# Low weight parts of the search stage made by GpSimd alone, and four re-orderings around it

## The chip, the cores and the metric

The kernel is one program on one core of a Trainium2 chip. The time is the device time of an execution in microseconds (us). TensorE (PE, with its weight loads PEld), VectorE (DVE), ScalarE (ACT), GpSimd (POOL) and SyncE (SP, which only issues DMAs here) each run their own instructions in order and wait for each other through semaphores.

## The reference

Two layers of a token model, 256 tokens by 1024 features, all in float32. Layer 0 has a gated MLP (w_in, w_out), layer 1 a pooling mixer (p_in, p_out); each is followed by an expert block. Cut to what matters:

```
mod = silu(c) @ ada_w[i] + ada_b[i]              # 6 chunks: shift, scale, gate, twice
h   = rmsnorm(x) * gain * (1 + scale) + shift
q   = h @ w_q                                    # 1024 -> 8 heads x 2 x 128
s1, s2 = q_half1 @ k1.T, q_half2 @ k2.T          # 128 scores each
v1, i1 = top_k(s1, 16);  v2, i2 = top_k(s2, 16)
best, pos = top_k(v1[:, None] + v2[None, :], 16) # experts i1 * 128 + i2
out = sum_k gelu(h . u[e_k]) * softmax(best)_k * v[e_k]
```

The kernel computes gelu(h . u[e]) for all 16384 experts, masks the result with the gates of the chosen ones, and multiplies with all of v.

## The kernel before

All weights stream through TensorE as tiles of 128 x 1024 float32 (512 KB), in the order w_v, w_u, w_out, w_q, u, v for layer 0 and p_in, p_out, w_q, u, v for layer 1. A product runs in a reduced float32 form, so each tile is split: `wH` is ScalarE's copy of `raw` (line 403), `wL = raw - wH` is the low part. In most stages VectorE makes the first half of `wL` (`low_first`, line 627) and GpSimd the second (`low_second`, line 382); in the second band of u and in v VectorE makes it whole (`low_tile`, line 633). `raw`, `wH` and `wL` have four buffers each: SyncE loads tile n when TensorE has finished tile n - 4. ScalarE copies three tiles ahead, VectorE two (`ahead`, `ahead_whole`). TensorE's `tile_product` (lines 1185 to 1187) takes 24 matmuls for a tile: wH by hH, wH by hL, wL by hH for each of 8 k; `first_two` (lines 1200 to 1202) is the same for the first two tiles of a stage, right behind a norm.

**The front.** 16 tiles of ada_w are scaled by silu(c) and added on VectorE (`ada_front`, lines 646 and 649), eight for the scale chunk and eight for the shift chunk. TensorE sums the partitions (`modulations`, line 1228) and takes the mean square of x (`mean`, line 1218). `inverse_root` is line 686, `scaled` line 689, `low_h` line 694. The other chunks' 80 tiles of ada_w are loaded and added among later stages; `ADA_W_V` and `ADA_W_OUT` say behind which tiles.

**The search.** u has 128 tiles in two bands of 64. During the first band VectorE searches the best keys and experts: 66 steps (`topk_step`), of which 0 to 22 search single scores, 23 to 38 the sums C (line 934 makes C), 39 and 40 convert, 41 to 64 are eight groups of two products and a sum (lines 960, 968, 970) and 65 normalises the gates. `share` gives each step a price and spreads the steps between the `low_first` of the 64 tiles. ScalarE takes the exponential behind tile 52, TensorE transposes the result ahead of tile 60 (`stage(..., 60, BAND)`).

**The bands.** In the second band of u, and in the first half of v, VectorE, ScalarE and TensorE also mask the first and second band of results R (`gate_step`, `multiply`, line 1013). A masked tile of R is split in its turn: `gateH` on ScalarE (line 555, `split_gated`) and `gateL` on VectorE (line 1110, `low_gated`), both of which `values` needs for a v tile.

Of the kernel before, what the change touches and what calls it, by code (L numbers as in the profile page):

```python
# [27 lines left out]
KT = D // P  # L28
# [14 lines left out]
EXP_TILES = KEYS  # L43
RAW = 4
# [19 lines left out]
def build(nc, xt_d, c_d, ada_d, adab_d, n1_d, n2_d, fg_d, w_in_d, vg_d, ws_d, bs_d, w_out_d, p_in_d, p_grp_d,  # L64
# [13 lines left out]
    with ctx:  # L78
# [127 lines left out]
        s_low = sem("s_low")  # L206
        s_pe = sem("s_pe")
# [65 lines left out]
        ADA_W_OUT = tuple(t for t in range(4, 16) if t % 3 != 0)  # L273
# [6 lines left out]
        HALVES = (0, BASE["p_in", 1] - BASE["u", 0] - BAND)  # L280
        WHOLE = (BASE["u", 0] + BAND, BASE["u", 1] + BAND - (BASE["p_in", 1] - BASE["u", 0] - BAND))
# [3 lines left out]
        def _(sp):  # L285
# [34 lines left out]
            for t in range(16):  # L320
                load(stream_dram["w_u", 0], W_U, t // 4, t % 4)
                if t < 4:
                    load_ada(ada_s, m)
                    m += 1
# [43 lines left out]
        def _(pool):  # L368
# [15 lines left out]

            for layer in range(LAYERS):
                base, end = (0, BASE["p_in", 1])[layer], BASE["u", layer] + BAND
                with pool.Fori(0, (end - base) // 4) as i:
                    for s in range(4):
                        low_second(layer, base, i, s)
                if layer == 0:  # L390
# [8 lines left out]
        def _(act):  # L399
# [40 lines left out]
            nc.scalar.activation(csT[:, :], csT[:, :], ACT.Silu).then_inc(s_silu, 1)  # L440
            act.wait_ge(s_x, 16)
# [4 lines left out]
            for layer in range(LAYERS):  # L446
# [74 lines left out]
                experts(0, 52)  # L521
# [3 lines left out]
                experts(52, BAND)  # L525
# [85 lines left out]
        def _(dve):  # L611
# [148 lines left out]
            for layer in range(LAYERS):  # L760
                if layer == 0:
# [27 lines left out]
                    for t in range(16):  # L789
                        ahead(W_U, t // 4, t % 4)  # L790
                        if t < 4:
# [124 lines left out]
                for t in range(16):  # L916
                    ahead(BASE["w_q", layer], t // 4, t % 4)
# [124 lines left out]
                def share(n):  # L1042

                    if n < 39:
                        return (17, 24)[n > 22] + (14 if n == 0 else 28 if n in (23, 31) else 0)
                    return 12 if n < 41 or n == 65 else (7, 7, 12)[(n - 41) % 3]

                base = BASE["u", layer]
                made = 0
# [20 lines left out]
                dve.wait_ge(s_bank_a, 4 + ACT_EVACS + ACT_PER_LAYER * layer + 16 + BAND)  # L1070
                def whole_sum(i, s):
# [34 lines left out]
                def low_gated(i, s):  # L1106

                    dve.wait_ge(s_gH2, 4 * i + (layer * EXP_TILES + s + 1))
                    gated = ds(4 * i + s, 1)
                    nc.vector.tensor_tensor(gateL[s % 4][:, :],  # L1110
# [58 lines left out]
        def _(pe):  # L1169
# [100 lines left out]
            for j in range(KT):  # L1270
                mean(0, j)
# [240 lines left out]
```

## Time and profile before

| | us |
|---|---|
| median of 3 runs | 1999.16 (1992.68 to 2001.68) |
| profiled execution | 2005.55 |
| its span, first to last instruction | 2003.8 |
| TensorE busy in the span | 1920.3 |
| mean granted TensorE clock | 0.979 of full speed |

The profiled execution is 6.4 us over the median of the runs, and 1.75 us of it lie outside the span. All times below count from the start of the span. A matmul's time in the trace overlaps with the next one's, so a group's mean is longer than its pace.

### The profile page before, as it was taken

What the parts mean: (1) busy time and instruction counts of PE and PEld (TensorE: products, weight loads), DVE (VectorE), ACT (ScalarE), POOL (GpSimd) and SP (SyncE); (2) the same over time, 40 slices, a digit from 0 to 9 for tenths busy, and PEclk for the clock granted to TensorE, in tenths of its full rate; (3) what the DMA queues carried; (4) which work ended last, traced back from release to release, by engine and by line L of the source; (5) the groups of instructions that cost most, each with busy time, mean ns of one, the idle gap of its engine ahead of it and who ended that gap; (6) DMA issues with size and microseconds to landing.
All of it is one profiled execution on the core that took longest, in us unless ns stands there. A gap on an engine that the chain in (4) does not pass through costs nothing.

```text
span 2003.8 us, 40366 instructions
## 1 busy us (share of the span) xinstructions
PE 1920.3 (96%) x14140; PEld 1717.9 (86%) x14140; DVE 1597.5 (80%) x2713; ACT 921.1 (46%) x1470; POOL 346.6 (17%) x237
## 2 busy tenths in 40 slices
PE   3999899999999999999999899999999999999998
PEld 3999899999888888878888899999888878887886
DVE  7757588997998888888996558897898888886555
ACT  3464344454454444444543344444555544444454
POOL 1544344441000000000002344444000000000000
PEclk8999899999999999999997999999999999999999
DMA  7846345556554455568883335555664445545553
GB/s 285 314 158 232 125 150 185 170 168 203 197 184 160 151 167 167 167 229 318 323 302 116 127 137 168 178 177 169 210 201 157 166 156 167 167 166 177 194 189 136
DMA packets 104179, 376.38 MB, mean 188 GB/s; under 512 B 12464, under 2 KB 12464, under 8 KB 103856
## 3 DMA queue, kind: packets, MB, share of 16 engines
q1 hardware_dynamic: 103680, 373.43, 54.8%
q0 software_dynamic: 432, 2.10, 0.3%
q8 instruction: 38, 0.62, 0.1%
q14 instruction: 29, 0.24, 0.0%
HBM read 374.43 MB, written 1.05 MB: 187 GB/s over the span
## 4 chain that ended last, share of the span: by engine, by line
PE 84%; DVE 8%; DMA 4%; ACT 1%; issue 1%; SPq 0%; DVEq 0%; ACTq 0%
PE ring L1381 12%; PE O L1415 12%; PE O L1417 11%; PE O L1416 11%; PE ring L1185 8%; PE ring L1187 7%; PE ring L1186 7%; PE ring L1383 6%; PE ring L1357 2%; PE O L1357 2%; DVE wL L627 2%; DMA raw<-in_u 1%; PE O L1228 1%; PE O L1218 1%; DMA raw<-in_v 1%
## 5 line engine op out<-in xcount | busy, mean ns | idle before, releaser
L403 ACT ACTIVATE wH<-raw 128x1024 fp32r<-128x1024 f32 x608 | 644.8, 1061 | 982.2 <-DMA raw<-in_v 397.2
L633 DVE TENSOR_TENSOR wL<-raw,wH 128x1024 fp32r<-128x1024 f32 x384 | 469.8, 1223 | 195.4 <-ACT wH L403 193.3
L1185 PE MATMUL ring<-hX,wH 128*128 128x256 f32 x1536 | 444.6, 289 | 11.0 <-DVE wL L627 11.0
L1186 PE MATMUL ring<-hX,wH 128*128 128x256 f32 x1536 | 437.6, 285 | 0.0
L1187 PE MATMUL ring<-hX,wL 128*128 128x256 f32 x1536 | 437.5, 285 | 0.0
L382 POOL TENSOR_TENSOR wL<-raw,wH 128x512 fp32r<-128x512 f32 x224 | 343.7, 1536 | 466.7 <-ACT wH L403 466.5
L1415 PE MATMUL O<-wH,gateH 128*128 128x512 f32 x1024 | 408.4, 399 | 7.0 <-DVE gateL L1110 6.8
L1417 PE MATMUL O<-wH,gateL 128*128 128x512 f32 x1024 | 401.7, 392 | 0.0
L1416 PE MATMUL O<-wL,gateH 128*128 128x512 f32 x1024 | 400.7, 391 | 0.0
L1381 PE MATMUL ring<-hX,wH 128*128 128x512 f32 x1024 | 367.9, 402 | 0.0
L1185 PEld LDWEIGHTS ring<-hX,wH 128*128 128x128 f32 x1536 | 296.8, 193 | 14.7 <-DVE wL L627 10.9
L1186 PEld LDWEIGHTS ring<-hX,wH 128*128 128x128 f32 x1536 | 296.7, 193 | 0.1
L1187 PEld LDWEIGHTS ring<-hX,wL 128*128 128x128 f32 x1536 | 296.4, 193 | 0.0
L627 DVE TENSOR_TENSOR wL<-raw,wH 128x512 fp32r<-128x512 f32 x224 | 204.5, 917 | 108.2 <-ACT wH L403 107.1
L1383 PE MATMUL ring<-hX,wL 128*128 128x256 f32 x1024 | 287.2, 280 | 0.0
L1415 PEld LDWEIGHTS O<-wH,gateH 128*128 128x128 f32 x1024 | 193.6, 189 | 47.4 <-DVE gateL L1110 5.2
L1381 PEld LDWEIGHTS ring<-hX,wH 128*128 128x128 f32 x1024 | 192.7, 188 | 42.7
L1417 PEld LDWEIGHTS O<-wH,gateL 128*128 128x128 f32 x1024 | 193.4, 189 | 41.4
L1416 PEld LDWEIGHTS O<-wL,gateH 128*128 128x128 f32 x1024 | 194.0, 189 | 38.6
L1383 PEld LDWEIGHTS ring<-hX,wL 128*128 128x128 f32 x1024 | 194.0, 189 | 0.0
L1004 DVE TENSOR_TENSOR oneA<-oneE,selG 128x1536 bf16<-128x1536 bf16 x128 | 121.7, 951 | 0.3
L1110 DVE TENSOR_TENSOR gateL<-R,gateH 128x256 fp32r<-128x256 f32 x256 | 106.4, 417 | 7.2 <-ACT gateH L555 7.2
(168 smaller groups left out, 1952.9 us busy)
## 6 DMA issues: line engine op xcount, KB each, us to landing
raw<-in_u SPq DMA_DIRECT2D x256, 512.0 KB, 3.3
raw<-in_v SPq DMA_DIRECT2D x256, 512.0 KB, 3.3
ada_v<-in_ada SPq DMA_DIRECT2D x40, 512.0 KB, 4.7
raw<-in_w_in SPq DMA_DIRECT2D x32, 512.0 KB, 4.1
raw<-in_w_q SPq DMA_DIRECT2D x32, 512.0 KB, 3.3
ada_f<-in_ada SPq DMA_DIRECT2D x16, 512.0 KB, 10.5
ada_s<-in_ada SPq DMA_DIRECT2D x16, 512.0 KB, 4.8
raw<-in_w_out SPq DMA_DIRECT2D x16, 512.0 KB, 3.5
```

The lines of the kernel that those rows point to most:

```text
L382: nc.gpsimd.tensor_tensor(wL[s % RAW][:, HALF:], raw[s % RAW][:, HALF:], wH[s % RAW][:, HALF:].bitcast(fp32), ALU.subtract).then_inc(s_l1, 1)
L403: nc.scalar.activation(wH[s % RAW][:, :], raw[s % RAW][:, :], ACT.Copy).then_inc(s_h, 1)
L627: nc.vector.tensor_tensor(wL[s % RAW][:, 0:HALF], raw[s % RAW][:, 0:HALF], wH[s % RAW][:, 0:HALF].bitcast(fp32), ALU.subtract).then_inc(s_ ...
L633: nc.vector.tensor_tensor(wL[s % RAW][:, :], raw[s % RAW][:, :], wH[s % RAW][:, :].bitcast(fp32), ALU.subtract).then_inc(s_low, 1)
L1185: mm(bank[:, 0:T], a, xH[:, k0 + k, :], start=(first and k == 0), stop=False)
L1186: mm(bank[:, 0:T], a, xL[:, k0 + k, :], start=False, stop=False)
L1187: ins = mm(bank[:, 0:T], b, xH[:, k0 + k, :], start=False, stop=(last and k == KT - 1))
L1381: mm(bank[:, :], wH[s][:, k * P:k * P + P], hX[:, k, :, :].rearrange("p two t -> p (two t)"), start=(k == 0), stop=False)
L1383: ins = mm(bank[:, 0:T], wL[s][:, k * P:k * P + P], hH[:, k, :], start=False, stop=(k == KT - 1))
L1415: mm(o[:, :], a, high, start=first, stop=False)
L1416: mm(o[:, :], a, low, start=False, stop=False)
L1417: ins = mm(o[:, :], b, high, start=False, stop=last)
```

## The change

The diff, cut to its core:

```diff
-        ADA_W_OUT = tuple(t for t in range(4, 16) if t % 3 != 0)
+        ADA_W_OUT = (4, 5, 7, 8)
+        SEARCH = 48
@@ sync and vector, in the w_u stage: four more ada tiles @@
-                if t < 4:
+                if t < 8:
@@ gpsimd @@
+            pool.wait_ge(s_acc, ADA_FRONT)
+            def low_whole(base, i, s):
+                pool.wait_ge(s_h, 4 * i + (base + s + 1))
+                nc.gpsimd.tensor_tensor(wL[s % RAW][:, :], raw[s % RAW][:, :], wH[s % RAW][:, :].bitcast(fp32),
+                                        ALU.subtract).then_inc(s_low_p, 1)
             for layer in range(LAYERS):
-                base, end = (0, BASE["p_in", 1])[layer], BASE["u", layer] + BAND
+                base, end = (0, BASE["p_in", 1])[layer], BASE["u", layer]
                 (low_second for tiles base to end, as before)
+                with pool.Fori(0, SEARCH // 4) as i:
+                    for s in range(4):
+                        low_whole(end, i, s)
@@ scalar: front, exponential, end of the second band @@
             nc.scalar.activation(csT[:, :], csT[:, :], ACT.Silu).then_inc(s_silu, 1)
+            act.wait_ge(s_const, 6)
+            warm_root()
...
-                experts(0, 52)
+                experts(0, 40)
                 act.wait_ge(s_diff, layer + 1)
                 nc.scalar.activation(best[:, :, :, :], ex[:, :, :, :], ACT.Exp).then_inc(s_exp, 1)
                 warm()
-                experts(52, BAND)
+                experts(40, BAND)
...
                 for s in range(4):
-                    act.wait_ge(s_sum, BAND * layer + 4 * last + s)
-                    ahead(BASE["u", layer] + BAND, last, s)
-                    gelu(last, s - 1)
                     if s == 3:
                         act.wait_ge(s_gated, NGRP * (2 * layer + 1))
                         split_gated(0, 0, first=True)
                         split_gated(0, 1, first=True)
+                    act.wait_ge(s_sum, BAND * layer + 4 * last + s)
+                    gelu(last, s - 1)
+                    ahead(BASE["u", layer] + BAND, last, s)
@@ vector: front @@
             modulations(1, (1,), O[3], (0,))
+            for m in range(KT + 3, ADA_FRONT):
+                ada_front(m)
             dve.wait_ge(s_x, 16)
             inverse_root(0)
-            for m in range(KT + 3, ADA_FRONT):
-                ada_front(m)
@@ vector: w_q and search @@
-                    ahead(BASE["w_q", layer], t // 4, t % 4)
+                    if t < 14:
+                        ahead(BASE["w_q", layer], t // 4, t % 4)
...
-                for n in range(BAND):
-                    if n < BAND - 2:
-                        ahead(base, n // 4, n % 4)
-                    else:
-                        ahead_whole(base, n // 4, n % 4)
-                    while made < 66 and sum(share(x) for x in range(made + 1)) <= 19 * (n + 2):
-                        topk_step(made)
-                        made += 1
+                for n in range(66):
+                    topk_step(n)
+                for n in range(SEARCH - 2, BAND):
+                    ahead_whole(base, n // 4, n % 4)
@@ vector: end of the second band, then of v's first half @@
                 for s in range(4):
+                    if s == 3:
+                        whole_sum(PAIRS - 1, s - 1)
+                        low_gated(0, 0)
+                        low_gated(0, 1)
                     ahead_whole(base + BAND, PAIRS - 1, s)
-                    whole_sum(PAIRS - 1, s - 1)
-                    gate_step(PAIRS - 1, s, 0, last=True)
+                    if s < 3:
+                        whole_sum(PAIRS - 1, s - 1)
+                        gate_step(PAIRS - 1, s, 0, last=True)
-                low_gated(0, 0)
-                low_gated(0, 1)
...
                     else:
+                        if s == 3:
+                            low_gated(PAIRS, 0)
                         ahead_whole(base, PAIRS - 1, s)
                     gate_step(PAIRS - 1, s, 1, last=True)
-                low_gated(PAIRS, 0)
                 low_gated(PAIRS, 1)
@@ tensor: front, search stage @@
+            modulations(acc_f, 0, 1, KT, O[3])
             for j in range(KT):
                 mean(0, j)
-            modulations(acc_f, 0, 1, KT, O[3])
             modulations(acc_f, 1, 2, ADA_FRONT, O[3][:, KT:])
...
-                stage("u", layer, s_bank_a, before, 0, 60)
+                stage("u", layer, s_bank_a, before, 0, SEARCH, by_pool=layer)
+                stage("u", layer, s_bank_a, before, SEARCH, 60, whole=layer)
...
-                stage("u", layer, s_bank_a, before, 60, BAND)
+                stage("u", layer, s_bank_a, before, 60, BAND, whole=layer)
```

With `by_pool` and `whole`, `tile_product` waits once for the whole low part, where it waited for each half. The constants that count the semaphores follow.

First place, VectorE in the front, before. `acc_f` are the sums of ada_w, `rstd` the inverse root, `sq` the scaled x:

```order
L649 SCALAR_TENSOR_TENSOR acc_f<-ada_f,csT,acc_f 128x1024 x2
L675 TENSOR_TENSOR mod<-O,adab 128x8
L679 SCALAR_TENSOR_TENSOR gs<-mod,n 128x8
L682 MEMSET tick 128x1
L686 RECIPROCAL rstd<-std 128x256
L649 SCALAR_TENSOR_TENSOR acc_f<-ada_f,csT,acc_f 128x1024 x5
L689 SCALAR_TENSOR_TENSOR sq<-XT,gs,rstd 128x256 x4
```

The same place of the changed kernel:

```order
L664 SCALAR_TENSOR_TENSOR acc_f<-ada_f,csT,acc_f 128x1024 x2
L690 TENSOR_TENSOR mod<-O,adab 128x8
L694 SCALAR_TENSOR_TENSOR gs<-mod,n 128x8
L697 MEMSET tick 128x1
L664 SCALAR_TENSOR_TENSOR acc_f<-ada_f,csT,acc_f 128x1024 x5
L701 RECIPROCAL rstd<-std 128x256
L704 SCALAR_TENSOR_TENSOR sq<-XT,gs,rstd 128x256 x4
```

The reciprocal stands behind the last five sums, where it stood ahead of them.

Second place, VectorE in the search, layer 0, before; `M` is the comparison matrix of steps 41 to 64:

```order
L627 TENSOR_TENSOR wL<-raw,wH 128x512
L960 TENSOR_TENSOR M<-ab,iota_b 128x1024
L968 TENSOR_TENSOR M<-M,top_f 128x1024
L627 TENSOR_TENSOR wL<-raw,wH 128x512
L970 TENSOR_REDUCE sel<-M 128x64
L960 TENSOR_TENSOR M<-ab,iota_b 128x1024
```

The last such group of the changed kernel and what follows it:

```order
L984 TENSOR_TENSOR M<-M,top_f 128x1024
L986 TENSOR_REDUCE sel<-M 128x64
L991 TENSOR_REDUCE zsum<-best 128x16
L992 RECIPROCAL zsum<-zsum 128x16
L993 TENSOR_TENSOR sel<-best,zsum 128x256
L648 TENSOR_TENSOR wL<-raw,wH 128x1024 x17
L1069 CAST selK<-O 128x512 x2
```

The low parts are gone from between the steps, and whole ones come in a row behind the last step.

Third place, VectorE at the end of the second band, before. Line 1075 is `whole_sum`:

```order
L1013 TENSOR_TENSOR R<-O,R 128x64x8 x2
L633 TENSOR_TENSOR wL<-raw,wH 128x1024
L1075 TENSOR_TENSOR R<-ring,R 128x256
L1110 TENSOR_TENSOR gateL<-R,gateH 128x256 x2
L1075 TENSOR_TENSOR R<-ring,R 128x256
```

And changed:

```order
L1029 TENSOR_TENSOR R<-O,R 128x64x8 x2
L1088 TENSOR_TENSOR R<-ring,R 128x256
L1080 TENSOR_TENSOR gateL<-R,gateH 128x256 x2
L648 TENSOR_TENSOR wL<-raw,wH 128x1024
L1088 TENSOR_TENSOR R<-ring,R 128x256
```

The two `gateL` stand ahead of the last low part of the band, where they stood behind it.

## Rows read from the trace of the kernel before

**Rows 1.** The page's first part: busy time, share of the span and instructions of each engine.
```profile
PE 1920.3 (96%) x14140; PEld 1717.9 (86%) x14140; DVE 1597.5 (80%) x2713; ACT 921.1 (46%) x1470; POOL 346.6 (17%) x237
```

**Rows 2.** TensorE's waits over the span: us in total, times, longest us.
```profile
PE ring L1185 <- DVE wL L627: 13.2, 16, 2.2
PE O L1228 <- DVE acc_f L649: 11.7, 1, 11.7
PE O L1415 <- DVE gateL L1110: 6.8, 4, 2.4
```

**Rows 3.** TensorE's waits in 300:480, then in 1210:1400.
```profile
PE ring L1185 <- DVE wL L627: 4.5, 6, 1.2
...
PE ring L1185 <- DVE wL L627: 4.2, 5, 1.2
```

**Rows 4.** Timeline of 205:214, TensorE at the end of w_out.
```profile
210.17 1.92 PE L1228 MATMUL O<-ones,acc_s 128*128 128x1 f32 x16 [1.67 <-DVE acc_s L649]
```

**Rows 5.** Timeline of 18:43: start us, us, engine, line, work, [idle before].
```profile
19.94 2.67 DVE L649 SCALAR_TENSOR_TENSOR acc_f<-ada_f,csT,acc_f 128x1024 f32<-128x1024 f32 x2 [0.52 <-DMA ada_f<-in_ada]
...
25.63 1.75 DVE L686 RECIPROCAL rstd<-std 128x256 f32<-128x256 f32 x1
27.41 9.38 DVE L649 SCALAR_TENSOR_TENSOR acc_f<-ada_f,csT,acc_f 128x1024 f32<-128x1024 f32 x5
...
30.04 5.68 POOL L382 TENSOR_TENSOR wL<-raw,wH 128x512 fp32r<-128x512 f32 x3 [28.16 <-ACT wH L403]
...
36.72 1.66 DVE L689 SCALAR_TENSOR_TENSOR sq<-XT,gs,rstd 128x256 f32<-128x256 f32 x4
...
36.85 3.57 PE L1228 MATMUL O<-ones,acc_f 128*128 128x1 f32 x16 [11.75 <-DVE acc_f L649]
38.31 1.28 DVE L627 TENSOR_TENSOR wL<-raw,wH 128x512 fp32r<-128x512 f32 x2
...
42.03 0.55 PE L1200 MATMUL ring<-hX,wH 128*128 128x256 f32 x1 [1.60 <-DVE hX L694]
```

**Rows 6.** Busy time in windows: 286:343; 277:445; 277:445, VectorE's L627 alone; 107:121.
```profile
286.00:343.00 57.00, 57.00 (x477) 57.00 (x476) 52.53 (x188) 26.61 (x41) 26.47 (x20) 1.00 0.55 184
...
277.00:445.00 168.00, 163.54 (x1335) 162.01 (x1335) 149.85 (x396) 77.47 (x116) 78.75 (x56) 0.99 0.51 169
...
277.00:445.00 168.00, 51.07 (x55) 0.99 0.51 169
...
107.00:121.00 14.00, 14.00 (x121) 14.00 (x120) 4.40 (x5) 10.58 (x23) 7.25 (x5) 1.00 0.50 161
```

**Rows 7.** Timeline of 674:680, where the second band ends in layer 0.
```profile
674.05 1.28 DVE L1013 TENSOR_TENSOR R<-O,R 128x512 f32<-128x512 f32 x2
...
678.67 0.71 ACT L555 ACTIVATE gateH<-R 128x256 fp32r<-128x256 f32 x2
```

**Rows 8.** Timeline: GpSimd alone, then beside VectorE, from 355 on.
```profile
358.45 1.30 POOL L382 TENSOR_TENSOR wL<-raw,wH 128x512 fp32r<-128x512 f32 x1 [1.43 <-ACT wH L403]
...
438.33 1.84 POOL L382 TENSOR_TENSOR wL<-raw,wH 128x512 fp32r<-128x512 f32 x1 [3.17 <-ACT wH L403]
...
438.32 0.69 DVE L960 TENSOR_TENSOR M<-ab,iota_b 128x1024 bf16<-128x1024 bf16 x1
439.05 1.67 DVE L627 TENSOR_TENSOR wL<-raw,wH 128x512 fp32r<-128x512 f32 x1
```

**Rows 9.** The page: ScalarE's weight copies (part 5) and the loads (part 6).
```profile
L403 ACT ACTIVATE wH<-raw 128x1024 fp32r<-128x1024 f32 x608 | 644.8, 1061 | 982.2 <-DMA raw<-in_v 397.2
...
raw<-in_u SPq DMA_DIRECT2D x256, 512.0 KB, 3.3
```

**Rows 10.** VectorE's groups by shape in 268:455: busy us, mean ns | idle before.
```profile
L970 DVE TENSOR_REDUCE sel<-M 128x64 f32<-128x1024 bf16 x8 | 9.7, 1214 | 0.1
...
L934 DVE TENSOR_TENSOR C<-top_v 128x2048 f32<-128x2048 f32 x2 | 6.8, 3384 | 0.0
```

**Rows 11.** Timeline of ScalarE in 279:295: the result of the search's first tile leaves.
```profile
282.01 0.38 ACT L516 ACTIVATE R<-ring 128x256 f32 x1 [2.81 <-PE ring L1187]
```

More of the change, by code:

```diff
@@ L206, in build @@
         s_low = sem("s_low")
+        s_low_p = sem("s_low_p")
         s_pe = sem("s_pe")
@@ L277, in build @@
         ACT_PER_LAYER = 16 + EXP_TILES
-        HALVES = (0, BASE["p_in", 1] - BASE["u", 0] - BAND)
-        WHOLE = (BASE["u", 0] + BAND, BASE["u", 1] + BAND - (BASE["p_in", 1] - BASE["u", 0] - BAND))
+        SEARCH = 48
+        HALVES = (0, BASE["p_in", 1] - BASE["u", 0])
+        BY_POOL = (BASE["u", 0], BASE["u", 1] - SEARCH)
+        WHOLE = (BASE["u", 0] + SEARCH, BASE["u", 1] + SEARCH - (BASE["p_in", 1] - BASE["u", 0] - SEARCH))
         @block.sync
@@ L790, in _ @@
                         ahead(W_U, t // 4, t % 4)
-                        if t < 4:
+                        if t < 8:
                             ada_tile(ada_s, acc_s, m // KT - 2, m)
@@ L1040, in gate_step @@
                         multiply(i, 0, band)
[L1042 to L1046, printed above, removed]
                 base = BASE["u", layer]
-                made = 0
-                for n in range(BAND):
-                    if n < BAND - 2:
-                        ahead(base, n // 4, n % 4)
-                    else:
-                        ahead_whole(base, n // 4, n % 4)
-                    while made < 66 and sum(share(x) for x in range(made + 1)) <= 19 * (n + 2):
-                        topk_step(made)
-                        made += 1
+                for n in range(66):
+                    topk_step(n)
+                for n in range(SEARCH - 2, BAND):
+                    ahead_whole(base, n // 4, n % 4)
                     if n == 62:
@@ L1070, in _, with low_gated @@
                 dve.wait_ge(s_bank_a, 4 + ACT_EVACS + ACT_PER_LAYER * layer + 16 + BAND)
+                def low_gated(i, s):
+                    dve.wait_ge(s_gH2, 4 * i + (layer * EXP_TILES + s + 1))
+                    gated = ds(4 * i + s, 1)
+                    nc.vector.tensor_tensor(gateL[s % 4][:, :],
+                                            R[:, gated, :].rearrange("p a t -> p (a t)"),
+                                            gateH[s % 4][:, :].bitcast(fp32), ALU.subtract).then_inc(s_gL2, 1)
                 def whole_sum(i, s):
@@ L1099, in _ @@
                 for s in range(4):
+                    if s == 3:
+                        whole_sum(PAIRS - 1, s - 1)
+                        low_gated(0, 0)
+                        low_gated(0, 1)
                     ahead_whole(base + BAND, PAIRS - 1, s)
-                    whole_sum(PAIRS - 1, s - 1)
-                    gate_step(PAIRS - 1, s, 0, last=True)
+                    if s < 3:
+                        whole_sum(PAIRS - 1, s - 1)
+                        gate_step(PAIRS - 1, s, 0, last=True)
                 base = BASE["v", layer]
[L1106 to L1110, printed above, removed]
-                                            R[:, gated, :].rearrange("p a t -> p (a t)"),
-                                            gateH[s % 4][:, :].bitcast(fp32), ALU.subtract).then_inc(s_gL2, 1)
                 def ahead_gated(i, s):
@@ L1170, in _, with tile_product @@
             mm = nc.tensor.matmul
-            def tile_product(base, i, s, bank, xH, xL, k0=0, first=True, last=True, pairs=None, whole=None):
+            def tile_product(base, i, s, bank, xH, xL, k0=0, first=True, last=True, pairs=None, whole=None, by_pool=None):
                 if whole is not None:
                     pe.wait_ge(s_low, 4 * i + (base - WHOLE[whole] + s + 1))
+                if by_pool is not None:
+                    pe.wait_ge(s_low_p, 4 * i + (base - BY_POOL[by_pool] + s + 1))
                 for k in range(KT):
-                    if whole is None and k % 4 == 0:
+                    if whole is None and by_pool is None and k % 4 == 0:
                         pe.wait_ge((s_l0, s_l1)[k // 4], 4 * i + (base - HALVES[base >= BASE["p_in", 1]] + s + 1))
@@ L1204, in first_two, with stage @@
                             ins.then_inc(s_pe, 1)
-            def stage(name, layer, emptied, before, lo=0, hi=None):
+            def stage(name, layer, emptied, before, lo=0, hi=None, **made):
                 base = BASE[name, layer]
@@ L1212, in stage @@
                         pe.wait_ge(emptied, 4 * i + (before + s + 1))
-                        tile_product(base, i, s, ring[s], hH, hL)
+                        tile_product(base, i, s, ring[s], hH, hL, **made)
             def mean(n, j):
```

## The prediction

> **What bounds the kernel now.** I read the page first: TensorE is busy 1920.3 us of the span [rows 1], so the most that any re-ordering can give is the 83 us in which it stands. Then TensorE's waits, to see whom it waits for: VectorE's half low parts 13.2 us in 16 waits, the front's sums of ada_w 11.7 us in one, `gateL` 6.8 us in four [rows 2]. The same view by stretch puts 4.5 us of the low-part waits into the search of layer 0 and 4.2 us into that of layer 1 [rows 3]; the rest is in w_v, w_u and w_out, where the low parts stay as they are. Last the timelines around those waits. The change touches 11.7 + 6.8 + 8.7 us of waiting, and a 1.67 us wait at the end of w_out [rows 4].
>
> **The front.** Before, VectorE takes the reciprocal at 25.63, five sums from 27.41 (9.38 us), four scaled tiles (1.66), two low halves (1.28); TensorE's second sums over partitions run from 36.85 for 3.57 and end at 40.42, and the first product starts 1.61 later, at 42.03 [rows 5]. The five sums took 1.88 each, where the two before them took 1.33: GpSimd's three halves of 30.04 to 35.72 lay beside them [rows 5]. After: TensorE sums the scale chunk while it would wait for x, so VectorE goes on at 22.6 (19.94 + 2.67) with 0.5 of small operations, ends five undisturbed sums at 23.1 + 5 x 1.39 = 30.05 (1.33 and a gap), then reciprocal 1.75, scaled 1.66, low halves 1.28: 34.7. GpSimd now starts at 30.05, by its new wait, so its three halves (3.9 alone) lie beside the scaled tiles and the low halves. What VectorE loses to it is bounded by nothing and by all 3.9; I take 1.9, since the reciprocal has one input and ran undisturbed, and half of GpSimd's work falls there. That is 36.6. TensorE's second sums end at 30.05 + 3.57 = 33.6, ahead of it. The first product starts at 36.6 + 1.6 = 38.2 and the front gains 3.8, between 1.8 and 5.7. The mean squares start some 2.5 us later than before, but the root is not asked for until 30.05: no cost. The square-root table is loaded early, off the path too.
>
> **The sums spread.** Four additions move from w_out to w_u. In 107:121 VectorE is busy 4.40 of 14 us [rows 6]; four sums at 1.3 to 2.3 us add 5 to 9 us there and fit. Their four loads move with them on SyncE's queue, each behind a weight load and each waiting for an earlier sum; the next weight load stands behind that wait, and it is short as long as VectorE has this room. At the end of w_out TensorE stops at 208.5 and starts its sums at 210.17, 1.67 later [rows 4]; with the additions done long before, it goes straight on: 1.7 gained. If the cover in w_u fails, each sum holds up a low half by up to 1 us: 0 to 2 us lost; I take 0.
>
> **The gate tiles.** At the end of the second band both masks are done at 674.05 + 1.28 = 675.3, but ScalarE makes `gateH` only at 678.67, behind a weight copy that waits for its load [rows 7]. After, ScalarE waits for the masks first, with the last weight copy of the stage behind that wait, and they are done before it gets there: `gateH` follows at about 675.9 and `gateL` at 676.7; TensorE ends its tile at 677.4, so the whole wait goes. The low part behind it is done at 678.3, and TensorE wants it one v tile later, at 680. In the middle of v `gateL` is made ahead of a low part that waits for ScalarE. All four waits go: 6.8 gained.
>
> **The search.** Removed: 48 of VectorE's halves per layer, and with them the waits of [rows 3], 8.7 us. Added: GpSimd makes 48 whole parts. Is it fast enough? TensorE does 477 matmuls in 57 us, so a tile of 24 takes 2.87 [rows 6]. GpSimd's half takes 1.30 alone [rows 8]; a whole one lies between 1.30 (nothing for more columns) and 2.60 (twice), and near the latter: I take 2.45, since some of 1.30 is start-up. The Trainium skill, page "GPSIMD Engine Reference", section 3.1, gives about 2.6 cycles at 1.2 GHz per element for a two-input operation, 2.2 us here as an estimate and some start-up, which would leave the sum as it is, and it says to leave elementwise work to VectorE; no run here yet shows a whole tile. So GpSimd keeps up by 0.4 us a tile. The latency: a tile's load starts when TensorE is four tiles ahead, and three tiles (8.6 us) later it is wanted. Load 3.3, copy 1.06 [rows 9], GpSimd 2.45 and some 0.5 of hand-over make 7.3: a slack of 1.3.
>
> What eats it is the port that GpSimd and VectorE share in operations with two inputs. At 438.3 VectorE's M product and GpSimd's half start together: GpSimd takes 1.84 in place of 1.30; then VectorE's next, of 0.69 alone, takes 1.67 and ends 0.55 after GpSimd's end [rows 8]. One waits for the other, and about 0.13 us of each overlap. In steps 41 to 64 there are 16 M products. A GpSimd tile and one of them take 2.45 - 0.13 + 0.55 = 2.87 per tile: GpSimd just holds TensorE's pace, and VectorE gets one product in per tile. Price: 0.2 to 0.5 us for each of the two C products (3.4 us [rows 10], against a slack of 1.3), about 0.3 for ScalarE's exponential behind tile 40, 0 to 1.5 for the M products. By the Trainium skill, "SBUF — State Buffer", section "SBUF: two separate sides", the pair is an exclusive lock for the whole instruction; without the overlap a pair would take 3.14, GpSimd would fall back 16 x 0.27 = 4.3 us, and 3 us a layer would come back as waits. The trace agrees that one blocks the other, with the 0.13 less at each end.
>
> Is VectorE in time for tile 48, which it makes itself? Its work in 277:445 is 149.85, less 51.07 for low halves 98.8 [rows 6], and about 5 more to the last step: 104 us from 277 on. The M products wait for GpSimd's tiles: 16 x 2.87 = 46 us, where eight groups of 0.69 + 0.69 + 1.21 [rows 8, 10] take 21; that adds 25, the conversions ahead of them about 5. The last step ends at about 411, between 406 and 417. Tile 0 ends at about 282.0 [rows 11], so tile 48 is wanted at 282.0 + 47 x 2.87 = 416.9, and its part must start by 415.7. It holds, by little; a miss costs 0 to 2 us. In all I give back 1.3 us a layer: the search gains 8.7 - 2.6 = 6.1, between 0 and 8.7.
>
> **The sum.** 3.8 + 1.7 + 6.8 + 6.1 = 18.4 us. The profiled execution of 2005.55 would be 1987.2; the median of the runs, 6.4 lower, goes from 1999.16 to 1980.8.
>
> **The rivals.**
> Port: the lock costs GpSimd and VectorE more than I took: a pair of whole tile and M product takes 3.1 us or more, and the search ends behind tile 48. Then waits of 4 to 5 us a layer come back, in the last third of the first band, the search gains nothing, and 12.3 us remain: 1986.9. For it: the two estimates above are both within 1 to 5 us of tipping. Against: the pair in the rows, and GpSimd's 0.4 us of room wherever no such product comes.
> Front: all of GpSimd's 3.9 us stand in VectorE's way, and the front gives 1.8 only: 16.4 in all, 1982.8. This lies within the likeliest case's range.
> GpSimd too slow, the one on the other side: a whole low part takes more than a tile of TensorE, and 96 tiles pay the difference. The rest gains 12.3 and the removed waits 8.7, so it breaks even at 2.87 + 21/96 = 3.09 and at 3.3 the kernel is 20 us slower: 2019. For it: the 56 halves of 277:445 took 1.41 each [rows 6], and twice that is 2.81, 0.06 short of a tile. Against: those include halves that stood beside VectorE's own half, which is no longer there; alone it is 1.30 [rows 8].
> Nothing: the waits only move to the next semaphore. Every engine behind them (loads 3.3 us, copies 1.06) has more slack than the waits are long, so I give it little: within 5 us of before, 1996.
>
> **Chances.** Likeliest 0.66 (1974 to 1988), port 0.20, GpSimd too slow 0.07, nothing 0.07. 0.5% is 10 us, about what a measurement of this kernel can tell from no change (its three runs spread over 9 us). Faster by more: the first two cases, less the part of them above 1989: 0.80. Slower: the part of the third beyond 3.2 us a tile: 0.05. The rest, 0.15, is no change. The range takes in the first two cases and the width of the runs: 1971 to 1991.
>
> **What would show it.** GpSimd's whole parts at 2.4 to 2.6 us alone and 2.9 to 3.1 beside M products; the M products at up to 3 us each; waits of TensorE in the search under 3 us a layer; no wait for `gateL`; the first product at about 38 us; no wait for `acc_s` at the end of w_out. Wrong would be: GpSimd busy without a gap through tiles 0 to 47 and TensorE waiting for it tile by tile; or a wait of more than 3 us at tile 48.

## The result and the profile after

The changed kernel takes 1971.35 us (median of four runs, 1968.64 to 1976.10) against 1999.41 of the kernel before: a ratio of 0.9871, interval 0.9847 to 0.9896. A repetition in another call gave 1970.78 and 0.9864 (0.9844 to 0.9884). The profiled execution went from 2005.55 to 1976.1, its span from 2003.8 to 1973.9. The forecast was 1980.8, 9.4 us above the median: the medians gained 28.1 us where 18.4 were forecast. All four terms have the right sign.

TensorE's waits over the span, in the columns of [rows 2]:

```profile
PE O L1239 <- DVE acc_f L664: 20.3, 2, 17.2
PE ring L1211 <- DVE hX L709: 16.8, 4, 4.4
PE O L1275 <- ACT UV L522: 5.9, 6, 2.0
PE ring L1196 <- DVE wL L642: 2.6, 2, 2.1
...
PE O L1229 <- ACT sq L423: 1.6, 1, 1.6
PE ring L1196 <- POOL wL L392: 0.8, 2, 0.5
```

The 13.2 us for VectorE's low halves have become 2.6, 2.1 of it at the start of w_out, GpSimd's whole parts (`low_whole`, L392) cost 0.8, and `gateL` and `acc_s` are gone. The 20.3 for `acc_f` isn't new time: its 17.2 lies at the start, where TensorE waited for x before. The page has TensorE busy for 1914.6 us, 5.7 less than in [rows 1], with as many matmuls; a re-ordering alone does not explain that, and it is followed up below.

The front (timeline of 19:43), beside [rows 5]:

```profile
23.23 6.84 DVE L664 SCALAR_TENSOR_TENSOR acc_f<-ada_f,csT,acc_f 128x1024 f32<-128x1024 f32 x5
...
29.99 1.75 DVE L701 RECIPROCAL rstd<-std 128x256 f32<-128x256 f32 x1
30.13 3.58 PE L1239 MATMUL O<-ones,acc_f 128*128 128x1 f32 x16 [3.15 <-DVE acc_f L664]
30.32 3.92 POOL L385 TENSOR_TENSOR wL<-raw,wH 128x512 fp32r<-128x512 f32 x3 [28.43 <-ACT wH L416]
...
31.77 3.54 DVE L704 SCALAR_TENSOR_TENSOR sq<-XT,gs,rstd 128x256 f32<-128x256 f32 x4
35.24 1.28 DVE L642 TENSOR_TENSOR wL<-raw,wH 128x512 fp32r<-128x512 f32 x2
...
38.00 0.55 PE L1211 MATMUL ring<-hX,wH 128*128 128x256 f32 x1 [4.29 <-DVE hX L709]
```

The five sums take 6.84 in place of 9.38 and end at 30.07 (forecast 30.05). The scaled tiles take 3.54, 1.88 more than the 1.66 of [rows 5], because GpSimd's 3.92 lie beside them (forecast 1.9), and the first product starts at 38.00 (forecast 38.2).

The search in layer 0: GpSimd's parts (min/median/max ns, first and last start), then VectorE's groups in 362:406 (busy us, mean ns), then the timeline, GpSimd beside the last M products and VectorE where the search ends:

```profile
L392 POOL TENSOR_TENSOR wL<-raw,wH x47: 2363/2411/4445, 263.6 to 404.0; 128x1024 fp32r<-128x1024 f32 x47
```
```profile
L984 DVE TENSOR_TENSOR M<-M,top_f 128x1024 bf16<-128x1024 bf16 x8 | 20.2, 2519 | 0.3
L976 DVE TENSOR_TENSOR M<-ab,iota_b 128x1024 bf16<-128x1024 bf16 x8 | 12.6, 1570 | 0.3
L986 DVE TENSOR_REDUCE sel<-M 128x64 f32<-128x1024 bf16 x8 | 9.8, 1220 | 0.3
```
```profile
393.14 13.67 POOL L392 TENSOR_TENSOR wL<-raw,wH 128x1024 fp32r<-128x1024 f32 x5 [2.04 <-ACT wH L416]
...
406.57 0.52 DVE L993 TENSOR_TENSOR sel<-best,zsum 128x256 f32<-128x256 f32 x1
407.01 1.22 DVE L648 TENSOR_TENSOR wL<-raw,wH 128x1024 fp32r<-128x1024 f32 x1
```

GpSimd's whole part takes 2.41 us where nothing hinders it (taken: 2.45). The Trainium skill's 2.2 us and some start-up (page "GPSIMD Engine Reference", section 3.1, an estimate from its cycles per element) agrees. Of two M products, 0.69 each when alone [rows 8], one takes 1.57 and the other 2.52 on average: VectorE pays more for the port than GpSimd. The last step ends at 407.09 (forecast 411, bounds 406 to 417).

**Where the time came from.** I cut every execution at the same events: the starts of ScalarE's table loads, and the start of norm 1's root. "experts0" and "experts1" are the stretches with u and v, search included, of layer 0 and layer 1. The rows of the repetition of the changed kernel (timeline of ScalarE):

```profile
40.59 1.28 ACT L447 ACT_TABLE_LOAD   x1
...
155.17 1.28 ACT L450 ACT_TABLE_LOAD   x1
...
266.85 1.28 ACT L447 ACT_TABLE_LOAD   x1
...
1040.45 1.28 ACT L450 ACT_TABLE_LOAD   x1
...
1187.68 1.28 ACT L447 ACT_TABLE_LOAD   x1
...
1950.09 1.28 ACT L450 ACT_TABLE_LOAD   x1
```

The lengths between them, in us. "Low clock" is what TensorE lost below its full clock after 40 us, summed from windows of 4 us as busy time x (1 - granted clock), windows at 0.985 or more left out. A time "cleared of the clock" is a length less this sum over its windows:

```
                   front w_v,w_u  w_out  to u  experts0 between experts1   span  low clock
before, recorded    44.4  118.1   50.7   63.5   784.8    149.1   773.1   2003.8   28.7
before, repeated    45.5  116.1   51.7   62.2   782.3    146.4   772.0   1996.1   18.0
after, recorded     40.4  116.2   48.6   62.9   773.7    150.0   762.0   1973.9   23.8
after, repeated     40.6  114.6   48.8   62.9   773.6    147.2   762.4   1969.9   16.5
e1 gate tiles old   40.6  113.6   48.9   63.0   776.6    146.8   766.5   1975.9   18.0
e2 search old       40.6  113.6   48.7   63.3   779.0    145.0   766.7   1976.8   15.2
e3 front old        44.7  114.1   48.8   63.2   773.0    146.8   762.6   1972.9   18.2
e4 sums old         40.6  113.4   51.6   62.4   773.2    145.6   762.3   1969.0   15.0
e10 front+sums old  43.6  114.8   51.6   63.8   774.0    145.9   763.5   1977.1   19.0
```

Two executions of one kernel differ by 10.7 and 7.3 us in the last column alone, and the 5.7 us of TensorE's busy time above are mostly its 4.9. Without it the recorded pair gains 2003.8 - 28.7 - (1973.9 - 23.8) = 25.0 and the repeated one 1996.1 - 18.0 - (1969.9 - 16.5) = 24.7. That they agree so well is chance: with the low clock off, the two executions of before still differ by 3.0 us and those of the changed kernel by 3.3, and the pairs taken crosswise give 21.7 and 28.0. So the gain is 25 us, give or take 3, against a sum of 18.4.

### The profile page after: what moved, and what is told of

Same layout as the page of the kernel before. It is cut to its first block, busy times and chain, and to the rows that moved or that the text cites. A ratio compares the mean times of both kernels' runs of the same rounds, so it can differ in the third digit from the quotient of the medians.

```text
span 1973.9 us, 40165 instructions
## 1 busy us (share of the span) xinstructions
PE 1914.6 (97%) x14140; PEld 1716.5 (87%) x14140; DVE 1572.1 (80%) x2617; ACT 921.8 (47%) x1471; POOL 404.5 (20%) x205
## 4 chain that ended last, share of the span: by engine, by line
PE 60%; issue 19%; POOL 14%; DVE 3%; DMA 2%; ACT 1%; SPq 0%; POOLq 0%; DVEq 0%; ACTq 0%
PE O L1427 12%; PE O L1429 11%; PE O L1428 11%; PE ring L1393 10%; POOL wL L392 9%; POOL wL L385 6%; PE ring L1395 5%; PE ring L1368 2%; PE ring L1196 2%; PE ring L1197 2%; PE ring L1198 2%; PE O L1368 2%; DMA raw<-in_u 1%; ACT wH L416 1%; DVE wL L648 1%
## 5 line engine op out<-in xcount | busy, mean ns | idle before, releaser
L648 DVE TENSOR_TENSOR wL<-raw,wH 128x1024 fp32r<-128x1024 f32 x416 | 508.7, 1223 | 232.0 <-ACT wH L416 230.8
L392 POOL TENSOR_TENSOR wL<-raw,wH 128x1024 fp32r<-128x1024 f32 x96 | 246.3, 2576 | 47.1 <-ACT wH L416 46.7
L1428 PEld LDWEIGHTS O<-wL,gateH 128*128 128x128 f32 x1024 | 193.0, 188 | 38.2
L385 POOL TENSOR_TENSOR wL<-raw,wH 128x512 fp32r<-128x512 f32 x96 | 155.3, 1621 | 254.6 <-ACT wH L416 254.6
L642 DVE TENSOR_TENSOR wL<-raw,wH 128x512 fp32r<-128x512 f32 x96 | 88.0, 920 | 67.1 <-ACT wH L416 66.9
```

The costliest lines, as they stand in the source:

```text
L385: nc.gpsimd.tensor_tensor(wL[s % RAW][:, HALF:], raw[s % RAW][:, HALF:], wH[s % RAW][:, HALF:].bitcast(fp32), ALU.subtract).then_inc(s_l1, 1)
L392: nc.gpsimd.tensor_tensor(wL[s % RAW][:, :], raw[s % RAW][:, :], wH[s % RAW][:, :].bitcast(fp32), ALU.subtract).then_inc(s_low_p, 1)
L648: nc.vector.tensor_tensor(wL[s % RAW][:, :], raw[s % RAW][:, :], wH[s % RAW][:, :].bitcast(fp32), ALU.subtract).then_inc(s_low, 1)
L1428: mm(o[:, :], a, low, start=False, stop=False)
```

## The experiments

Each is the changed kernel but for the edit shown. In the first group e1, e2, e3 and e4 put one part back and e10 two; e9 adds work to e1; r_before and r_after are the two kernels unchanged. The expected totals of e1, e2, e3 and e9 were counted from the recorded 1976.1, and the repetition's median is 1970.78, so they are some 5 us high by that alone. Above that median stand e1 by 7.6 us, e2 by 9.2, e3 by 5.2, e4 by 3.7 and e10 by 6.1. The ratios of e3, e4 and e10 overlap the repetition's, so what these cost is read from their rows and stretches.

**The parts, one by one.**

```diff
# e1 (VectorE; ScalarE's split_gated likewise behind its gelu)
-                    if s == 3:
-                        whole_sum(PAIRS - 1, s - 1)
-                        low_gated(0, 0)
-                        low_gated(0, 1)
...
+                low_gated(0, 0)
+                low_gated(0, 1)
```

> The changed kernel with the gate tiles back behind the weight copies (ScalarE and VectorE). Theory 'wait and clock': TensorE's four waits for gateL come back (2.2 to 2.4 us at the start of v, 1.0 to 1.2 in its middle, both layers, 6.8 in sum) and behind each of the two longer ones the granted clock falls to about 0.57 for 4 us, as in the trace of before, with some 12 matmuls in those 4 us where the changed kernel has 19 to 21: 1.7 us more a layer. Together 10 us: the profiled execution goes from 1976.1 to 1986 and the gain from the first v product to 8 tiles later is 1.7 smaller in each layer. Rival 'wait alone': the same waits, 6.8 us, 1983, and the clock at 1.00 in the first 4 us of v.

Measured: 1978.42 us, ratio 0.9913 (0.9895 to 0.9931). The waits, and the start of v in layer 0 (windows: busy times and matmul counts, granted clock after POOL):

```profile
PE O L1423 <- DVE gateL L1080: 6.7, 4, 2.4
```
```profile
659.00:663.00 4.00, 2.03 (x12) 1.53 (x10) 1.49 (x3) 2.18 (x6) 0.00 (x0) 1.00 0.53 161
663.00:667.00 4.00, 3.58 (x16) 2.97 (x17) 3.14 (x7) 2.88 (x7) 0.00 (x0) 1.00 0.21 85
```

The four waits are back with 6.7 us and the expert stages are 3.0 and 4.1 longer than the repetition's, 7.1 in all. Of the 3.0, 2.3 is low clock elsewhere in the stretch, where the repetition has none and the recorded execution 1.8; cleared of it, e1 costs 4.8 us against the repetition and 6.9 against the recorded execution. The clock behind the wait of 2.4 is 1.00, and so it is in layer 1. The rival holds: the wait alone.

```diff
# e9 = e1 and, ahead of the first v product
+                pe.wait_ge(s_h, base + 1)
+                for _ in range(9):
+                    mm(O[2][:, :], wH[0][:, 0:P], wH[0][:, 0:HALF], start=True, stop=True)
```

> The kernel of e1 with nine matmuls of 128x128x512 on the first v tile's own high part ahead of the first v product, so that TensorE is at work through the wait for gateL; they are started and stopped for themselves, and the product overwrites their bank. (Work is added, the result is the same.) Theory 'wait and clock': v still starts as late as in e1, but the clock stays at 1.00 in its first 4 us, so it is about 3.4 us faster than e1 (1982 to 1983 against 1986). Rival 'wait alone', the low rate of matmuls in those 4 us has another cause (low parts or banks): e9 is as long as e1, or 1 to 3 us longer.

Measured: 1985.81 us, ratio 0.9945 (0.9927 to 0.9963), 7.4 more than e1; the spans differ by 2.4 (1978.3 and 1975.9), and in them the expert stages (777.1 and 768.0) by 0.5 and 1.5, with waits for low parts of 1.5 us (VectorE's) and 1.3 (GpSimd's) that e1 has not. Two of the executions without a profile, 1986.0 and 1989.5 us, were granted 0.984 of the clock, where the profiled one of 1980.5 had 0.987. Keeping TensorE at work through the gap bought nothing, as there was no fall of the clock to avoid.

> The kernel before once more, unchanged, for its granted clock. In the recorded execution the clock stood at 0.57 in the 4 us behind both waits for gateL at the start of v (2.2 and 2.4 us long); in e1, with waits of 2.4 and 2.3 us at the same place, it stood at 1.00. Theory 'it follows from the kernel': 0.5 to 0.7 again in both layers here. Rival 'it varies from execution to execution, as the stretches behind the norms do (0.5 to 0.95 in the same places)': 1.00 in at least one of the two layers, and the time at low clock, 28.7 us of loss in the recorded execution, is 15 to 25 here.

The same windows, first of the recorded execution of before, then of this one:

```profile
676.00:680.00 4.00, 1.83 (x11) 1.35 (x10) 1.72 (x5) 2.24 (x5) 0.00 (x0) 1.00 0.52 187
680.00:684.00 4.00, 4.00 (x12) 3.13 (x11) 3.14 (x7) 1.98 (x4) 0.00 (x0) 0.57 0.04 17
684.00:688.00 4.00, 4.00 (x19) 3.31 (x18) 2.23 (x3) 0.71 (x2) 0.00 (x0) 1.00 0.37 131
```
```profile
673.00:677.00 4.00, 1.61 (x11) 1.17 (x9) 2.08 (x4) 2.95 (x8) 0.00 (x0) 1.00 0.53 179
677.00:681.00 4.00, 4.00 (x18) 3.33 (x19) 3.14 (x7) 2.43 (x6) 0.00 (x0) 1.00 0.09 38
```

The kernel and the gap (2.2 and 2.4 us) are the same; one execution falls to 0.57 and does 12 matmuls in 4 us, the other stays at 1.00 and does 18. The rival holds: it varies from execution to execution. That is 7/19 of 4 us or 1.5 in each layer of the recorded pair, which the change can save but doesn't always.

> The changed kernel once more, unchanged, on the chip of this call, to set the experiments against. Theory: the stretches between the landmarks (266 to 1042 and 1190 to 1956) repeat within 1 us (773.7 and 762.0 us), the ratio is 0.985 to 0.990, and the clock loss of 23.8 us in the recorded execution is smaller here by some us, since the four kernels of the first call showed 15 to 18. Rival: the clock loss is the same 24 and belongs to the kernel.

Measured: 773.6 and 762.4, within 0.4 us of the recorded ones; ratio 0.9864; loss at low clock 16.5. The theory holds.

```diff
# e2 (the pieces of it)
-        SEARCH = 48
-                with pool.Fori(0, SEARCH // 4) as i:
-                    for s in range(4):
-                        low_whole(end, i, s)
-                for n in range(66):
-                    topk_step(n)
+                    while made < 66 and sum(share(x) for x in range(made + 1)) <= 19 * (n + 2):
+                        topk_step(made)
+                        made += 1
```

> The changed kernel with the search as before: VectorE and GpSimd make a half of each low part each, and the search's steps lie between them by the table of shares. The prediction gave this part 6.1 us (8.7 of waits less 2.6 given back). The two traces give 4.8 in layer 0 and 5.5 in layer 1. Theory 'nothing is given back, and the removed waits cost more than their length': 9 to 11 us slower than the changed kernel, 1985 to 1987, with 4 to 5 us of waits for wL in each search. Rival 'the 6.1 of the prediction was right and the rest of the gain came from elsewhere in the stretch': 6 us slower, 1982.

Measured: 1979.97 us, ratio 0.9912 (0.9885 to 0.9938); expert stages 5.4 and 4.3 longer than in the repetition, 9.7 in all (cleared of the clock 8.4, and 10.5 against the recorded execution). TensorE's waits in 262:430, 1185:1350 and 1350:1410:

```profile
PE ring L1199 <- DVE wL L637: 4.7, 6, 0.9
...
PE ring L1199 <- DVE wL L637: 2.4, 3, 0.9
...
PE ring L1199 <- DVE wL L637: 1.2, 2, 0.7
```

These are 8.3 us, near the 8.7 of [rows 3]. The changed kernel pays 0.8 of it at most. So the part is worth 8 to 10 us and not 6.1: the theory holds, the forecast's give-back of 2.6 didn't come.

```diff
# e3 (VectorE; no wait of GpSimd for the sums; ScalarE and TensorE in the old order likewise)
-            for m in range(KT + 3, ADA_FRONT):
-                ada_front(m)
             dve.wait_ge(s_x, 16)
             inverse_root(0)
+            for m in range(KT + 3, ADA_FRONT):
+                ada_front(m)
# e4
-        ADA_W_OUT = (4, 5, 7, 8)
+        ADA_W_OUT = tuple(t for t in range(4, 16) if t % 3 != 0)
-                        if t < 8:
+                        if t < 4:
```

> The changed kernel with the front in its old order, on all four engines: GpSimd's halves beside the five sums, the reciprocal ahead of them, TensorE's scale chunk after the mean squares. Prediction: the first product 3.8 us later than in the changed kernel (41.8 against 38.0). The traces give 4.0. Rival, since layer 1 gave back 0.9 in its front: the front is worth only 3 by the end of the program. Total 1979 to 1980.

> The changed kernel with the eight modulation sums of w_out back in w_out (none of the four in w_u). Prediction: 1.7 us slower by the end of w_out, one wait for acc_s of about 1.7 us. The traces of before and after show 1.8 more in w_v and w_u, where low-part waits fell from 2.4 to 0.6. Theory A (these waits come from the sums too): 3 to 4 us slower by norm 1's root (landmark 205). Rival B (they come from something else, such as GpSimd's later start in the front): 1.7 slower, w_v and w_u unchanged.

> The changed kernel with front and modulation sums both as before, because 1.5 us of the gain in w_v and w_u (cleared of the granted clock) came back in no single experiment. Theory 'each alone hides it, both bring it': 40 to 157 (from the front's table load to that of w_out) takes 113.2 to 114.1 us cleared of the clock, as before, and not 111.3 to 112.0. Rival 'it belongs to neither': 111.3 to 112.0 again, and the whole kernel is the sum of e3 and e4, 4.1 + 2.8 = 6.9 us slower than the changed one.

Measured: e3 1976.0 us, ratio 0.9899 (0.9882 to 0.9917), front 4.1 longer, nothing else moved. e4 1974.44 us, 0.9889 (0.9866 to 0.9913), w_out 2.8 longer, and its wait is

```profile
PE O L1239 <- DVE acc_s L664: 1.9, 1, 1.9
```

with w_v and w_u as they are in the changed kernel: rival B. Its whole span is 0.9 shorter than the repetition's, within what two executions differ by, so the 2.8 rests on the stage alone. e10 1976.84 us, 0.9895 (0.9879 to 0.9912), front 3.0 and w_out 2.8 longer, the span 7.2. Its w_v and w_u take 114.8 less 2.5 at low clock, 112.3, between the 111.3 to 112.0 of the others and the 113.2 to 114.1 of before, so neither theory is met. No part that I put back brings this last 1 to 2 us whole.

**GpSimd's speed.**

```diff
# e7 (8 parts of 128 columns; the other run: 4 of 256)
-                nc.gpsimd.tensor_tensor(wL[s % RAW][:, :], raw[s % RAW][:, :], wH[s % RAW][:, :].bitcast(fp32),
-                                        ALU.subtract).then_inc(s_low_p, 1)
+                for q in range(0, KT * P, 128):
+                    ins = nc.gpsimd.tensor_tensor(wL[s % RAW][:, q:q + 128], raw[s % RAW][:, q:q + 128],
+                                                  wH[s % RAW][:, q:q + 128].bitcast(fp32), ALU.subtract)
+                ins.then_inc(s_low_p, 1)
```

> The changed kernel with each whole low part of GpSimd cut into four instructions of 256 columns (same result). From the rows, 512 columns take 1.30 and 1024 take 2.41, so 0.19 of it is start-up: four take about 2.95 us a tile, against 2.87 of TensorE. Theory 'GpSimd must stay below TensorE's tile, and every tile above it pays the difference' (the prediction's rival 'GpSimd too slow'): 96 x 0.08 = 8 us slower than the changed kernel less the lead it starts with (about 1 us a layer), so 5 to 8 us slower, with waits of TensorE for GpSimd's low parts in both searches. Rival 'the port's lock gives way between instructions, so shorter ones let VectorE in and the search keeps its time': within 2 us of the changed kernel.

> The same with eight instructions of 128 columns: by the rows 8 x 0.47 = 3.7 us a tile. Theory as above: 96 x 0.83 = 80 us slower less some us of lead, so about 2045, slower than the kernel before (the price per tile of the rival 'GpSimd too slow'); TensorE waits 0.8 us for GpSimd at each of 48 tiles a layer. If the start-up overlaps between instructions on one queue, the four and the eight parts both stay near 2.4 us a tile and both runs stay within 2 us of the changed kernel.

Measured: 1987.61 us, ratio 0.9952 (0.9936 to 0.9969), and 2038.11 us, ratio 1.0205 (1.0186 to 1.0225). GpSimd's group by shape, and TensorE's wait for it, of the four parts and then of the eight:

```profile
L393 POOL TENSOR_TENSOR wL<-raw,wH 128x256 fp32r<-128x256 f32 x384 | 292.7, 806 | 14.1 <-ACT wH L418 14.0
...
PE ring L1198 <- POOL wL L393: 13.6, 21, 1.1
```
```profile
L393 POOL TENSOR_TENSOR wL<-raw,wH 128x128 fp32r<-128x128 f32 x768 | 348.4, 500 | 8.1 <-ACT wH L418 8.0
...
PE ring L1198 <- POOL wL L393: 43.4, 78, 2.3
```

A tile takes GpSimd 292.7/96 = 3.05 us and 348.4/96 = 3.63. Against the 1970.78 of the repetition the kernel loses 16.8 and 67.3 us, so 50.5 us for 96 x 0.58 more: 0.91 for each us. The waits as listed come to only 13.6 and 43.4; why they cost more is worked out below. The line through the two points, an estimate, meets zero at 3.05 - 16.8/(96 x 0.91) = 2.86 us a tile, which is TensorE's 2.87 [rows 6], and meets the kernel before (1996.35 beside these runs, 25.6 above the repetition) at 3.15, where the forecast had 3.09. The theory holds; the expected 5 to 8 us for four parts was too low, since a tile took 0.10 more than it was sized at.

**GpSimd's start in the front.**

```diff
# e5
-            pool.wait_ge(s_acc, ADA_FRONT)
+            pool.wait_ge(s_xn, 4)
```

> The changed kernel with GpSimd's start behind the four scaled tiles instead of behind the sums. The prediction says that GpSimd's three halves cost VectorE's scaled tiles 1.9 us; the trace shows 3.54 for the four in place of 1.66. Theory 'this lies on the path': the scaled tiles take 1.7, the first product comes at 36.1 in place of 38.0, and the whole kernel is 1.9 us faster. Rival 'the port only moves the block': the three halves then lie beside the low half and the hX products, which are hidden or not; the first product at 37 to 38, and 0 to 1 us gained.

Measured: 1972.97 us, ratio 0.9882 (0.9857 to 0.9908), not told apart from the repetition. The timeline of 22:40:

```profile
31.97 1.67 DVE L704 SCALAR_TENSOR_TENSOR sq<-XT,gs,rstd 128x256 f32<-128x256 f32 x4
...
33.90 4.90 POOL L385 TENSOR_TENSOR wL<-raw,wH 128x512 fp32r<-128x512 f32 x3 [32.01 <-DVE sq L704]
...
35.06 1.19 DVE L704 SCALAR_TENSOR_TENSOR sq<-XT,gs,rstd 128x256 f32<-128x256 f32 x1
...
36.18 1.49 DVE L709 SCALAR_TENSOR_TENSOR hX<-sq,mod,hX 128x256 fp32r<-128x256 f32 x1
37.59 1.49 DVE L704 SCALAR_TENSOR_TENSOR sq<-XT,gs,rstd 128x256 f32<-128x256 f32 x1
37.81 0.55 PE L1211 MATMUL ring<-hX,wH 128*128 128x256 f32 x1 [3.91 <-DVE hX L709]
```

The scaled tiles are free again (1.67), and the operations behind them pay in their place: 1.19 and 1.49 for what takes 0.48 in the changed kernel. The first product gains 0.4 against the repetition's 38.20, and the table load behind the front comes 0.6 later (41.2 against 40.6). The rival holds: the block moves.

**A faster version.** The repetition shows two waits that the change left: 2.2 us at 157, where w_out's third tile stands behind VectorE's last low gates, and 2.5 us for `otok` at the end of layer 0, where ScalarE makes a last weight copy, which waits for its load, ahead of the copies of the output banks.

```diff
# b1 (VectorE, then ScalarE, the end of w_u)
+                        if f == 14:
+                            ahead(W_OUT, 0, 0)
...
+                    ahead(W_OUT, 0, 0)
                     act.wait_ge(s_small, SMALL)
                     warm_root()
# (ScalarE, the end of v)
-                    for s in (1, 2, 3):
+                    for s in (1, 2):
                         ahead(base, 31, s)
...
+                if layer < LAYERS - 1:
+                    ahead(base, 31, 3)
                 for j in range(KT):
                     act.wait_ge(s_res, KT * layer + j + 1)
```

> The changed kernel with the orders at two ends of stages changed. At the end of w_u VectorE makes the low half of the third w_out tile ahead of the last four low gates, and ScalarE makes the high part of the fourth ahead of its table load: TensorE's wait of 2.2 us at 157 should go, 1.5 to 2.2 us gained by norm 1 (landmark std). At the end of layer 0's v ScalarE copies the output banks ahead of its last weight copy, which waits for a load: the wait of 2.5 us for otok should fall to 1.2, 1 to 1.3 us gained by norm 2. Together 2.5 to 3.5 us less in the landmarks, 1967 to 1968. Rival: the moved half delays the low gates by 0.7, and TensorE waits for them instead: 0 to 1 us gained at w_out.

Measured: 1966.14 us, ratio 0.9855 (0.9833 to 0.9876), span 1964.2. TensorE's waits in 140:165 and 1038:1062, of the repetition and then of b1:

```profile
PE ring L1196 <- DVE wL L642: 2.2, 1, 2.2
...
PE ring L1464 <- ACT otok L616: 2.5, 1, 2.5
```
```profile
PE ring L1203 <- DVE wL L646: 0.6, 1, 0.6
...
PE ring L1471 <- ACT otok L618: 0.4, 1, 0.4
```

1.6 and 2.1 us of waiting are gone against the repetition; from the front's table load to norm 1's root it takes 162.2 us against 163.3, and experts0 770.3 against 773.6. The span is 5.7 shorter. The ratios of b1 and of the repetition overlap, so their times don't show b1 faster than the change. The wait at w_out is 1.7 to 2.2 us in every trace without this edit, so most of its 1.6 is shown to be the edit's; the stretch to norm 1 gave 1.1 where 1.5 to 2.2 was expected. The wait for `otok` is no such sign: of the unchanged kernel's two executions the recorded one has none, and e4 has 0.7. What the second edit brings isn't shown.

## Why the prediction was right, and where it was off

**The total.** The median of 1971.35 lies 0.35 us above the lower edge of the range and below the likeliest case, 1974 to 1988, and the repetition's 1970.78 is just outside the range. The kernel is faster for the reasons given, but the sum was too small by a third of what was gained, and that the median fell inside the range is luck.

**Front, 3.8.** Right in size and in working: 4.0 in the recorded pair, 4.1 by e3. Within it the 1.9 us for GpSimd beside the scaled tiles came as 1.88. The reciprocal's part rested on its one input alone, as no row of before has GpSimd beside it; in the changed kernel GpSimd is, from 30.32 on, and it takes the same 1.75. The Trainium skill's rule on the port ("SBUF — State Buffer", section "SBUF: two separate sides": one engine holds it for a whole instruction) agrees with 3.54 in place of 1.66, and with e5, where the same block appears further down.

**End of w_out, 1.7.** The wait was 1.9 in e4, and the stage grew by 2.8, 0.5 of it at low clock (2.0 in e4, 1.5 in the repetition); some 0.4 beyond wait and clock is unexplained.

**Gate tiles, 6.8.** 6.7 of waits by e1, and 7.1 us by length (4.8 to 6.9 cleared of the clock). What the step missed is the granted clock behind the gap in the recorded execution: 3 us more there, none in the repeated one.

**Search, 6.1.** 8 to 10 us are gained (e2), and both terms of the sum were off. The removed waits were priced at 8.7, their length as listed, and each costs more than that. TensorE at one of them, in the kernel before (timeline of 352:356):

```profile
353.59 0.28 PE L1187 MATMUL ring<-hX,wL 128*128 128x256 f32 x1
354.56 0.39 PE L1185 MATMUL ring<-hX,wH 128*128 128x256 f32 x1 [0.69 <-DVE wL L627]
354.78 0.28 PE L1186 MATMUL ring<-hX,wH 128*128 128x256 f32 x1
```

Without a wait these matmuls start 0.12 us apart. Here the starts are 0.97 and 0.22 apart, 0.95 more than twice 0.12, of which the trace lists 0.69: it counts from the modelled end of the matmul before, and the first step behind the wait is slow. Each of the 11 waits of [rows 3] costs 0.26 to 0.28 us more than listed, each of the 11 of e2 0.25 to 0.27, and the waits for GpSimd in e7 0.25 to 0.27 in the stretches 300:400. So the 11 waits cost 8.7 + 11 x 0.26 = 11.6 us. By the same count e2's are 8.3 + 2.9 = 11.2, and 13.6 and 43.4 of e7 become 19.1 and 63.7, near the 16.8 and 67.3 us that these runs lost.

The 2.6 given back came as 0.8 in two waits, 1.3 by this count, in the recorded execution, and 0.4 or 0.9 in the repetition. The larger of the two, 0.53 us at 314.11, stands behind GpSimd's longest part (4.45), which met a C product of 2.29. So 11.6 - 1.3 = 10.3 is what this step should have said. The price of a pair beside M products was nearly right: the five parts from 393.14 on took 13.67, and four products met them, so a meeting cost GpSimd 0.40 and a pair took 2.81, where 2.87 was taken; VectorE waited the rest. Turns without any overlap would be 2.41 + 0.69 = 3.10. "Port" needed 3.1 or more and was not met, though tile 48 was closer than forecast: VectorE ended its part at 408.23, and TensorE wanted it at 408.3 (an estimate: its first tile's result leaves at 273.39, and 47 tiles of 2.87 follow), or up to 1.3 later by the two waits before it.

**What no term had.** 1 to 2 us in w_v and w_u, where low parts were waited for in before for 2.4 us in the recorded and 1.0 in the repeated execution, and 0.6 and 0.7 after. Counted as above the removed ones are worth 2.5 us in the recorded pair and 0.5 in the repeated one; why they went stays open. And the clock: of the recorded 29.9 us, 4.9 are a difference in low clock (28.7 against 23.8).

Together, from the experiments: 4.1 + 2.8 + 7.1 + 9.7 = 23.7 us by length, and about 20 to 24 with the expert stages cleared of the clock, against 18.4 forecast and a measured 25, give or take 3. The rival "GpSimd too slow" was wrong on this chip's 2.41, but its arithmetic stands: e7 finds its break-even 0.06 us from where it was put. "Nothing" is excluded by e2: the waits went and nothing took their place.

## What to carry to other kernels

An engine that feeds another tile by tile cost next to nothing here below the fed engine's time a tile and nearly its whole excess beyond (0.91 of it, from two runs): size it by that one number, with what neighbours on a shared port do to it. A block by a shared port can't be scheduled away by a later start if the work behind it has two inputs as well; it moves to whoever is next. A wait's price is read from the starts of the instructions around it, not from the listed wait alone. Before a gain of 1% is put down to steps, take the same kernel's profile twice and subtract the time at low clock, which differed here by 10.7 us between two executions of one kernel; some 3 us of difference stayed even so.

## What the hardware showed unexpectedly

The granted clock behind the same gap of 2.2 to 2.4 us was 0.57 over 4 us (a mean between the levels 0.50, 1.2 GHz, and 1.00, 2.4 GHz) in both layers of one execution and 1.00 in both layers of two others (the repetition of before, and e1). Between GpSimd and VectorE the port wasn't shared evenly: GpSimd's part rose from 2.41 to about 2.81 beside an M product, the M product from 0.69 to 1.57 and 2.52 on average. Cutting GpSimd's part costs start-up each time: 2.41 us for 1024 columns at once, 14.69/21 x 4 = 2.80 for four of 256, and 10.50/25 x 8 = 3.36 for eight of 128, by the timelines of GpSimd ahead of 300 in the two runs of e7:

```profile
285.33 14.69 POOL L393 TENSOR_TENSOR wL<-raw,wH 128x256 fp32r<-128x256 f32 x21
```
```profile
289.56 10.50 POOL L393 TENSOR_TENSOR wL<-raw,wH 128x128 fp32r<-128x128 f32 x25
```
